# A two-network forward pass on one core: the mixers' list of steps in another order

## The reference, cut to what matters

```
h = rms_norm(x) * (1 + sc1) + sh1
p = h @ w_in                                # 19 columns of 128 for the branches, 32 for the gates
y_a = rwkv7(p[..])   # recurrence over time, done in 4 chunks of 64 tokens; layer norm; gate
y_b = spatial_gating(p[..]) ; y_c = short_conv(p[..])
y_d = s5(p[..])      # complex linear scan of 16 groups x 64 states, gelu, GLU product
merged = sum over n of sigmoid(gate_n) * y_n        # 4 branches
x = x + gt1 * (merged @ w_o)
x = x + gt2 * (relu(h2 @ ffn_w1) ** 2 @ ffn_w2)
```

## Time and profile before

| | us |
|---|---|
| median of 3 runs | 1161.66 (1161.2 to 1168.12) |
| profiled execution, its own time | 1161.85 |
| its span, first to last instruction | 1160.0 |
| mean granted TensorE clock | 0.976 |
| TensorE busy / VectorE / ScalarE | 1091.7 / 835.9 / 641.7 |

### The profile page before, as it was taken

The page is one execution under the profiler, slowest core; times in us unless marked ns, Lnnn a source line. Parts: engine busy times, 40 slices in busy tenths (PEclk is TensorE's granted clock), DMA queues, the critical chain, the costliest instruction groups (busy, mean ns, idle before and its releaser), DMA issues.

```text
span 1160.0 us, 21002 instructions
## 1 busy us (share of the span) xinstructions
PE 1091.7 (94%) x8588; PEld 1036.3 (89%) x8588; DVE 835.9 (72%) x1444; ACT 641.7 (55%) x1098; POOL 66.7 (6%) x79
## 2 busy tenths in 40 slices
PE   6996999999999979999999989899999979999996
PEld 6874999999987779999999978799989979999996
DVE  6465898887795397978787768998874587655442
ACT  6544576665564975756565675222333357875340
POOL 1130100000002001000000000000000011000010
PEclk9998999999999979999999989999999989999998
DMA  9366465556665844776776533222335255556551
GB/s 344 120 203 235 128 213 185 184 171 180 193 215 186 276 133 135 247 237 228 237 220 185 195 111 107 83 92 91 128 109 155 70 207 179 182 183 183 184 160 37
DMA packets 59857, 200.41 MB, mean 173 GB/s; under 512 B 6769, under 2 KB 11505, under 8 KB 59633
## 3 DMA queue, kind: packets, MB, share of 16 engines
q1 hardware_dynamic: 58032, 194.54, 51.7%
q10 hardware_dynamic: 1728, 4.53, 1.1%
HBM read 197.99 MB, written 1.05 MB: 172 GB/s over the span
## 4 chain that ended last, share of the span: by engine, by line
PE 81%; DVE 10%; ACT 6%; DMA 1%; issue 1%; ACTq 0%; SPq 0%; POOL 0%; DVEq 0%
PE ps L470 80%; DVE wlo L1552 2%; ACT whi L1037 1%; ACT L1037 1%; DVE xr L1558 1%; DMA ring<-pa_w_out 1%; DMA ring<-pa_w_in 1%; ACT xr L1037 1%; DVE cosT L1552 1%; ACT rr L1037 0%; DVE rst L1581 0%; DVE raw L1552 0%; DVE bks L1552 0%; DVE hl L1552 0%; ACT sc L1037 0%
## 5 line engine op out<-in xcount | busy, mean ns | idle before, releaser
L470 PE MATMUL ps<-hh,whi 128*128 128x256 f32 (+1 forms) x1656 | 481.1, 291 | 18.1 <-DVE wlo L1552 15.6
L470 PE MATMUL ps<-hh,wlo 128*128 128x256 f32 (+1 forms) x1656 | 471.3, 285 | 0.0
L470 PE MATMUL ps<-hl,whi 128*128 128x256 f32 (+1 forms) x1656 | 469.4, 283 | 0.0
L1552 DVE TENSOR_TENSOR wlo<-ring,whi 128x1024 fp32r<-128x1024 f32 (+1 forms) x313 | 376.1, 1216 | 73.8 <-ACT whi L1037 73.2
L1037 ACT ACTIVATE whi<-ring 128x1024 fp32r<-128x1024 f32 (+1 forms) x313 | 321.6, 1039 | 68.7 <-PE ps L470 52.6
L470 PEld LDWEIGHTS ps<-hh,whi 128*128 128x128 f32 x1656 | 316.6, 191 | 39.0 <-issue 31.2
L470 PEld LDWEIGHTS ps<-hl,whi 128*128 128x128 f32 x1656 | 317.1, 192 | 1.3 <-issue 1.0
L470 PEld LDWEIGHTS ps<-hh,wlo 128*128 128x128 f32 x1656 | 316.7, 191 | 0.0
L470 PE MATMUL ps<-hidh,whi 128*128 128x256 f32 x608 | 172.2, 283 | 0.0
L470 PE MATMUL ps<-hidh,wlo 128*128 128x256 f32 x608 | 172.1, 283 | 0.0
L470 PE MATMUL ps<-hidl,whi 128*128 128x256 f32 x608 | 172.1, 283 | 0.0
(11 more groups left out here) (360 smaller groups left out, 1354.3 us busy)
## 6 DMA issues: line engine op xcount, KB each, us to landing
ring<-ffn_w_in SPq DMA_DIRECT2D x88, 512.0 KB, 3.5
ring<-ffn_w SPq DMA_DIRECT2D x64, 512.0 KB, 4.4
ring<-w_in SPq DMA_DIRECT2D x51, 512.0 KB, 3.4
ring<-ada_w SPq DMA_DIRECT2D x48, 512.0 KB, 4.3
ring<-ffn_w_out SPq DMA_DIRECT2D x32, 448.0 KB, 3.3
ring<-rg_w_in SPq DMA_DIRECT2D x20, 512.0 KB, 4.4
ring<-pa_w_in SPq DMA_DIRECT2D x16, 512.0 KB, 7.5
ring<-ffn_w_out SPq DMA_DIRECT2D x16, 512.0 KB, 3.6
```

Of the source, the lines that this page charges most:

```text
L470: return e.matmul(o, l, r, start=start, stop=stop)
L1552: return e.tensor_tensor(o, a, b, op)
```

## The change

The same 90 entries stand in `PLAN` in another order, and eight entries `("Y", m)` are added, which do what stood behind the list.

1. Column 4 stands ahead of the first R step; column 14 ahead of the R step `bn`; `(0, 2)` ahead of the last G step.
2. Steps Q and X of a level stand side by side, one gate column to a level. The S steps i = 0 to 7 come behind the levels: 0 behind `(7, 2)`, followed at once by `U0` and R of chunk 0.
3. The three chunk steps and the S steps share the columns `(0, 1)` to `(2, 0)`; R of chunks 1, 2 and 3 stands right behind S steps 2, 4 and 6. The rest of the n = 0 gates and the layer norm come next, then all n = 3 merges.
4. `("Y", m)` stands behind `(m + 1, 3)`; the remainder `mgl` of block m is made one entry later than its rounding.

```diff
     for at in PLAN:
         if isinstance(at, int):
             whole("w_in", 8, (at,))
+        elif at[0] == "Y":
+            o.append(("yw", at[1], *YW[0]))
...
-    o.extend(("yw", m, *YW[0]) for m in range(8))
...
 PLAN = [
-    6, 2, 3, 0, 1, "R", 4, 5, "R", 17, 18, 7, 8, "R", 9, 10, "R", 11, "G", "R", 12, 13, "G", "R", 14, 15, 16, "G", "S", "R", "G", (0, 2),
-    "R", (1, 2), "R", "S", (2, 2), "R", (3, 2), "R", (4, 2), "R", "S", (5, 2), "R", (6, 2), "S", "R", (7, 2), "R", (0, 1), "S",
-    "R", (1, 1), "R", (2, 1), "S", "R", (3, 1), "R", (4, 1), "S", "R", (5, 1), "R", (6, 1), "S", "R", (7, 1),
-    "R", (0, 0), "S", "R", (1, 0), "R", (2, 0), "S", "R", (0, 3), "R", (1, 3), "R", (2, 3), "R", (3, 3), "R", (4, 3),
-    "R", (5, 3), "R", (6, 3), (7, 3), "R", (3, 0), (4, 0), "R", (5, 0), (6, 0), "R", (7, 0),
+    6, 2, 3, 0, 1, 4, "R", 5, "R", 17, 18, 7, 8, "R", 9, 10, "R", 11, "G", "R", 12, 13, "G", 14, "R", 15, 16, "G", "S", "R", (0, 2), "G",
+    "R", (1, 2), "R", (2, 2), "R", "R", (3, 2), "R", "R", (4, 2), "R", "R", (5, 2), "R", "R", (6, 2), "R", "R", (7, 2), "S", "R", "R",
+    (0, 1), "R", "S", (1, 1), "R", (2, 1), "S", "R", (3, 1), "R", "S", (4, 1), "R", (5, 1), "S", "R", (6, 1), "R", "S", (7, 1), "R",
+    (0, 0), "S", "R", (1, 0), "R", "S", (2, 0), "R", (3, 0), "R", "S", (4, 0), "R", (5, 0), "R", (6, 0), (7, 0),
+    (0, 3), (1, 3), ("Y", 0), (2, 3), ("Y", 1), (3, 3), ("Y", 2), (4, 3), ("Y", 3), (5, 3), ("Y", 4), (6, 3), ("Y", 5), (7, 3), ("Y", 6), ("Y", 7),
 ]
...
+                def gather_branches(m):
+                    c = number["yw", m, 0]
+                    g = ga[:, m, :]
+                    feed(c)
+                    through.wait_ge(e, c)
+                    mx_act.wait_ge(e, ("gate", m, 0))
+                    tt(g, ps[where["yw", m, 0]][:, 0:T], g, MUL).then_inc(*mx_dve.up(("prod", m, 0)))
+                    mx_dve.wait_ge(e)
+                    tt(g, g, pm[:, m, :], ADD).then_inc(*mx_dve.up(("merged", m)))
+                    for k in {0: (), 7: (6, 7)}.get(m, (m - 1,)):
+                        mx_act.wait_ge(e, ("mh", k))
+                        low_of(mgl[:, k, :], ga[:, k, :], mgh[:, k, :]).then_inc(*mx_dve.up(("ml", k)))
```

More of the change, by code:

```diff
@@ L409, in build @@
         gslot, turns, before, held = {}, 0, {}, [None] * 3
-        for m, n in (at for at in PLAN if isinstance(at, tuple)):
+        for m, n in (at for at in PLAN if isinstance(at, tuple) and at[0] != "Y"):
             if n:
@@ L994, in mixers @@
                         column(at)
+                    elif at[0] == "Y":
+                        y_of(at[1], 0)
                     elif isinstance(at, tuple):
@@ L998, in mixers @@
                         next(steps[at])
-                for m in range(8):
-                    y_of(m, 0)
                 residual(5, "w_o", 8, pair(mgh, mgl), lambda k: mx_dve.wait_ge(e, ("ml", k)))
@@ L1395, in merge @@
                         act(gt[j], ps[where["yw", m, n]][:, T:2 * T], ACT.Sigmoid).then_inc(*mx_act.up(("glu", m)))
+                def gather_branches(m):
+                    feed(number["yw", m, 0])
+                    mx_dve.wait_ge(e, ("merged", m))
+                    act(mgh[:, m, :], ga[:, m, :], ACT.Copy).then_inc(*mx_act.up(("mh", m)))
                 def sg():
@@ L1481, in mixers @@
                         column(at)
+                    elif at[0] == "Y":
+                        gather_branches(at[1])
                     elif isinstance(at, tuple):
@@ L1485, in mixers @@
                         next(steps[at])
[L1486 to L1490, removed]
                 residual(5, "w_o", 8)
@@ L2267, in mixers @@
                         next(steps[at])
[L2268 to L2278, removed]
                 residual(5, "w_o", 8)
```

## The result

| | before | after |
|---|---|---|
| median | 1161.2 us (5 runs) | 1170.75 us (5 runs, 1168.93 to 1172.03) |
| ratio, 95% interval | 1 | 1.0074 (1.0055 to 1.0092) |
| profiled execution | 1161.85 us | 1169.66 us |
| its span | 1160.0 us | 1167.8 us |

The change made the kernel slower by 0.7%, some 8.6 us. 1164.1 was forecast, with a range of 1154 to 1171 and 0.89 on "within 1%".

A forecast was written before the change was run, and what follows sets the result against it. The prediction took the stage's start as bound by ScalarE and VectorE, the middle by TensorE with VectorE close, the end by the `mgl` chain. Terms -9.0 + 0 + 4.4 + 4.9 + 1.4 - 0.9 + 1.5 = +2.3 gave 1164.1 us, range 1154 to 1171.

The forecast's parts named there:

- likeliest case: The forecast itself, the terms' sum of +2.3 us giving 1164.1 us; own range 1160 to 1168, chance 0.60.
- two signs of being wrong: No zeroing wait, or granted clock below 1.00 for over 10 us between the levels and the Y entries.
- Tail: Y entries among the last merges free TensorE's waits for `mgl` at `w_o`: -9.0 us, bounds -7.0 and -9.8.
- Levels side by side: Steps Q and X adjacent: ScalarE's copy of Q stays covered by the second half's products, 0 us.
- Zeroing: R of chunk 0 waits for VectorE's zeroing, queued behind S step 0: +4.4 us, bounds 3.6 and 5.2.
- S steps ahead of R: SA of chunks 1 to 3 waits for VectorE sums behind S steps 2, 4, 6: +4.9 us, bounds +2.4, +7.9.
- Head: Column 4 ahead of the first R step lengthens lora's wait for `lo` to 4.4 us: +1.4 us.
- Column 14 and (0, 2): They cover the waits at `bn` and for `gvT`, but VectorE is full; N step gains: -0.9 us, bounds 0, -2.6.
- Clock: New TensorE idle stretches cost one clock drop, a little shorter than 4.2 us: +1.5 us, bounds 0 and +13.5.
- Rival 2: Clock falls at each new gap, 4.5 us each: 1180.6 us with four gaps, 1171.6 with two; chance 0.08.
- Rival 1: Waits in the S stretch stay hidden as VectorE catches up: 1153.4 to 1158.5 us; chance 0.20.
- 3: Y entries don't free the tail, because VectorE reaches them late: 1173.1 us; chance 0.03.

The follow-up runs named there:

- e4: Kernel before, list kept to (2, 0), then n = 0 gates first, n = 3 merges behind with Y entries among the last; 1161.56 us, ratio 1.0001.
- e5: e4 with the Y entries one merge later and R of chunk 1 ahead of S step 7; 1153.98 us, ratio 0.9931.
- e1: Changed kernel with VectorE's zeroing of the state moved ahead of S step 0, to the end of step X of level 5; 1164.41 us, ratio 1.0026.
- e2: e1 with R of chunks 1, 2 and 3 ahead of S steps 2, 4 and 6; 1161.69 us, ratio 0.9996.
- e7: e2 with the eight S steps spread out, the first three among the levels; 1157.67 us, ratio 0.996.
- e3: Changed kernel with spare TensorE products of constants filling the waits at R of chunk 0 and SA of chunks 1 to 3; 1166.52 us, ratio 1.0046.
- e10: Changed kernel with the S step of S5's last output one column later, behind (4, 0); 1170.36 us, ratio 1.0069.
- e9: e5 with 6 spare products of constants on TensorE ahead of lora's wait; 1148.88 us, ratio 0.9884.
- e8: e7 with column 4 behind the first R step again; 1160.82 us, ratio 0.999.

## Why the prediction was right in its range and short in its size

The order of the terms, most of their sizes and the places where one would see them were right; +2.3 us was forecast, +7.8 came in the profiles and +8.6 in the runs' ratio. 1170.75 us lies 0.25 inside the upper edge of the range and outside the likeliest case's own 1160 to 1168, so the range held by luck. And of the prediction's two signs of being wrong one came true: between the levels and the Y entries the granted clock was down for 13.7 us, where 10 was the limit. The step that failed is the clock's term. Point by point:

- **Tail, -9.0: right.** `w_o` waits 1.09 us where 0.8 was counted, with full clock (1.00 in 947 to 960), so 9.8 - 1.1 = 8.7 us are won. e4 and e5 show that most of it can be had without the rest, if nothing new is put on the recurrence's end.
- **Levels side by side, 0: right.** No wait between Q and X in the trace after.
- **Zeroing, +4.4: right**, 4.27; e1 takes it back.
- **S steps ahead of R, +4.9: right**, 1.55 + 2.05 + 3.17 - 2.12 = 4.7 for 1.8 + 1.9 + 3.3 - 2.1. The prediction gave two reasons, the order of VectorE's queue and its 69 us of work beside 63. e2 tells them apart: the order is mended, and two thirds of the waits come back elsewhere; spreading the work mends that (e7).
- **Head, +1.4:** lora waits 4.27 where 4.4 was forecast; at the first G step 0.7 is left, the lower bound, since the slow stretch covers fewer columns.
- **Column 14 and (0, 2), -0.9:** -0.3. VectorE's chain decided, as said.
- **Clock, +1.5: this term was mis-sized.** It measured 5.1 us in the S and Y stretches (11.7 of 13.7 us at half clock with work under way), where one drop of 3.4 us had been taken for all the new waits. Three places fell, one of them for 6.8 us, and two of the three waits at SA were enough. Rival 2 had the mechanism right and each price (4.5 us) too high: 2.1, 1.5 and 1.5 us. e3 shows the cause.
- **Two terms were missing.** S step 0's input product (0.86 us) had stood in TensorE's wait before level 1 and cost nothing there; behind the levels it costs its full length. And the wait of 1.16 us for the bank that S5's outputs hold was not foreseen; e10 removes it.

On the clock, the trace of before had more to go by than the prediction's "one place of three". The tail has two waits more of about this length, and each is followed by products at the slow pace; this is one, the other is that of 1.86 us at 944.57:

```profile
934.35 0.58 PE L470 MATMUL ps<-mgh,whi 128*128 128x256 f32 x1 [2.15 <-DVE wlo L1552]
934.73 0.42 PE L470 MATMUL ps<-mgl,whi 128*128 128x256 f32 x1
934.95 0.42 PE L470 MATMUL ps<-mgh,wlo 128*128 128x256 f32 x1
```

With these, three of the six waits of about 2 us or more had a slow stretch behind them, where one stretch for all the new waits was taken.

Together: 0.4 at level 1 (with a slow stretch of 3.4 us behind the wait of 2.82 us at (0, 2)), 0.9, 4.3, 4.7, 5.1 and 1.2, less 8.7 for the tail, make 7.9 us. From the stage's first product the changed kernel took 9.0 us longer, and this execution was 1.2 us quicker before it (first product at 663.82 for 665.05), which is the 7.8 of the spans. 1.1 us are left over. My estimate for them: a wait costs some 0.2 us more than the idle time in its row (e10 took away 1.16 us of idle time and 1.3 us of the whole), and there are four waits more than before, 0.8 us; that is argued, not shown.

The list has 100 entries before and 108 after, not 90 as was written; the argument doesn't use the number. Rival 1 (waits stay hidden) and 3 (the tail not freed) are refuted by the trace.

Two rules had been weighed. In Perfetto Trace Analysis, section Optimization Strategy, the Trainium skill says that interleaving regimes may help. The runs agree: spreading the S steps gave 4.0 us (e7), and the order of before keeps all but the tail. In TensorE: Matmul & The Clock Gate, section Loop structure matters more than you think, the Trainium skill has a long wait ahead of each burst make it run cold. e3 and e9 agree by the clock, for waits of 2.0 to 4.3 us, but not each wait does it: the 1.55 us at SA of chunk 1 and the 3.26 us for `gvT` before were followed by none. The 0.08 given to rival 2 was too small a chance.

## What to carry to other kernels

Before two steps of a list are put side by side, look at what else stands in the queue of the engine that answers: a 0.27 us write behind a 5.6 us chain costs the chain. Count the VectorE work of the stretch, not only the order of its steps, and give each new wait the price of the clock stretch behind it, which here went from nothing (1.55 us) over half of the wait (2.1 us for 4.27) to twice its length (some 6 us for 2.82, in e8). And a part that gives 5 to 7 us can hide in a whole that gives nothing: undo parts one by one before the whole is thrown away; if a wait can't be shortened, filling it with spare products is worth a trial.

## What the runs showed of the hardware that was not expected

- Spare matmuls in a wait kept the clock up: 9, 3, 4 and 7 products in four waits brought 0.93 to 1.00 in the S stretch, and 6 in lora's wait ended a stretch of 10 us at 1.2 GHz and gave 5.1 us (e5 1153.98, e9 1148.88).
- Slow time inside a wait costs nothing: of 6.8 us at half clock around the zeroing's wait 4.8 counted, and e1 and e3 each got 2.1 to 2.2 us back for them.
- Neither whether a slow stretch follows nor its length is a function of the wait alone. After the same 2.8 us wait it was 3.5 us in e7 and 13.5 in e8; after the same 2.00 us wait at `bn` it was none in e5 and 3.4 us in e9. What sets it stays open here; a comparison of two orders carries such differences of up to 4 us in it.
